# A two-block transformer on one core: seven block products in place of eight in every second pair of feed-forward up slots

## The reference, cut to what matters

```python
def swiglu(x, w_gu, w_down):
    g, u = jnp.split(x @ w_gu, 2, axis=-1)
    return (jax.nn.silu(g) * u) @ w_down
...
    for i in range(DEPTH):
        h = h + 0.5 * swiglu(rmsnorm(h, ffn1_norm[i]), ffn1_w_gu[i], ffn1_w_down[i])
        ...
        h = h + 0.5 * swiglu(rmsnorm(h, ffn2_norm[i]), ffn2_w_gu[i], ffn2_w_down[i])
        ...
    for l in range(DEPTH_2):
        mod = jax.nn.silu(c) @ ada_w[l] + ada_b[l]
```

## Time and profile before

| | |
|---|---|
| median of three runs | 3028.4 us (3027.08 to 3031.49) |
| the profiled execution, its time | 3027.1 us |
| the profiled execution, its span | 3025.4 us |
| mean granted TensorE clock | 0.995 |
| PE matmul busy | 2989.9 us, 99% |
| DVE busy | 1691.3 us, 56% |
| ACT busy | 1104.4 us, 37% |
| POOL busy | 303.9 us, 10% |

### The profile page before, as it was taken

How to read it: one execution, slowest core, us unless ns; L and a number is a source line. 1 busy time by engine, 2 the same in 40 slices (tenths; PEclk the granted TensorE clock), 3 DMA queues, 4 the chain that set the end, 5 groups by cost and what they waited for, 6 DMA issues and landing times.

```text
span 3025.4 us, 36951 instructions
## 1 busy us (share of the span) xinstructions
PE 2989.9 (99%) x13582; PEld 2432.9 (80%) x13582; DVE 1691.3 (56%) x2381; ACT 1104.4 (37%) x1717; POOL 303.9 (10%) x248
## 2 busy tenths in 40 slices
PE   8999999999999999999999999999999999999999
PEld 7888888778888887888888888888888775688887
DVE  6655564565655557555456455555556767463334
ACT  4232333562332234322232454232323555552223
POOL 2000300000100012000030000200003215600000
PEclk9999999999999999999999999999999998999999
DMA  5332232123323223432232212333222420122232
GB/s 199 109 125 95 94 98 78 58 60 115 139 97 139 97 87 95 152 139 97 92 97 96 84 38 78 111 139 141 96 97 84 170 70 29 43 79 96 95 94 82
DMA packets 86804, 301.55 MB, mean 100 GB/s; under 512 B 10272, under 2 KB 19616, under 8 KB 85536
## 3 DMA queue, kind: packets, MB, share of 16 engines
q1 hardware_dynamic: 86688, 300.02, 30.0%
HBM read 297.88 MB, written 2.10 MB: 99 GB/s over the span
## 4 chain that ended last, share of the span: by engine, by line
PE 93%; DVE 3%; ACT 2%; POOL 1%; issue 1%; DMA 0%; DVEq 0%; SPq 0%; ACTq 0%
PE proj L1194 27%; PE proj L1196 27%; PE proj L1195 27%; PE ot L1341 1%; PE proj L1575 1%; PE proj L1577 1%; PE proj L1576 1%; DVE w_lo L1688 1%; PE sc L1575 1%; PE sc L1577 1%; PE sc L1576 1%; POOL work L644 1%; PE ot L1468 0%; PE tr L1301 0%; PE sc L1290 0%
## 5 line engine op out<-in xcount | busy, mean ns | idle before, releaser
L1194 PE MATMUL proj<-u_hi,w_hi 128*128 128x512 f32 x2632 | 1029.5, 391 | 13.6 <-DVE u_lo L1693 9.0
L1196 PE MATMUL proj<-u_hi,w_lo 128*128 128x512 f32 x2632 | 1021.6, 388 | 0.0
L1195 PE MATMUL proj<-u_lo,w_hi 128*128 128x512 f32 x2632 | 1021.6, 388 | 0.0
L1688 DVE TENSOR_TENSOR w_lo<-raw,w_hi 128x1024 fp32r<-128x1024 f32 (+4 forms) x567 | 657.2, 1162 | 492.1 <-ACT w_hi L673 482.9
L673 ACT ACTIVATE w_hi<-raw 128x1024 fp32r<-128x1024 f32 (+4 forms) x567 | 535.9, 954 | 334.9 <-PE proj L1196 212.9
L1194 PEld LDWEIGHTS proj<-u_hi,w_hi 128*128 128x128 f32 x2632 | 494.8, 188 | 122.8 <-issue 15.9
L1195 PEld LDWEIGHTS proj<-u_lo,w_hi 128*128 128x128 f32 x2632 | 495.0, 188 | 104.1 <-issue 3.1
L1196 PEld LDWEIGHTS proj<-u_hi,w_lo 128*128 128x128 f32 x2632 | 494.7, 188 | 101.9
L1194 PE MATMUL proj<-a_hi,w_hi 128*128 128x512 f32 x936 | 368.1, 393 | 3.4 <-DVE w_lo L1688 1.5
L1196 PE MATMUL proj<-a_hi,w_lo 128*128 128x512 f32 x936 | 364.9, 390 | 0.0
L1195 PE MATMUL proj<-a_lo,w_hi 128*128 128x512 f32 x936 | 364.5, 389 | 0.0
(11 more groups left out here) (469 smaller groups left out, 2879.7 us busy)
## 6 DMA issues: line engine op xcount, KB each, us to landing
raw<-in_ffn_gu SPq DMA_DIRECT2D x174, 512.0 KB, 3.4
raw<-in_in_w SPq DMA_DIRECT2D x68, 512.0 KB, 3.3
raw<-in_ffn_dn SPq DMA_DIRECT2D x64, 512.0 KB, 3.3
raw<-in_ff SPq DMA_DIRECT2D x64, 512.0 KB, 3.4
gate<-in_ada SPq DMA_DIRECT2D x8, 3072.0 KB, 12.0
raw<-in_ffn_dn SPq DMA_DIRECT2D x32, 384.0 KB, 3.0
raw<-in_in SPq DMA_DIRECT2D x18, 512.0 KB, 3.4
raw<-in_mla_out SPq DMA_DIRECT2D x16, 512.0 KB, 3.4
```

The costliest lines, as they stand in the source:

```text
L1194: pe.matmul(out, w_h, x_h, start=first, stop=False)
L1195: pe.matmul(out, w_h, x_l, start=False, stop=False)
L1196: return pe.matmul(out, w_l, x_h, start=False, stop=last)
L1688: dve.tensor_tensor(wt(w_lo, slot, slot.tiles), wt(raw, slot, slot.tiles), wt(w_hi, slot, slot.tiles).bitcast(F32), ALU.subtract).then_inc ...
```

## The change

Every second tile in the up rounds of the four blocks is worked as a 2x2 block product after Strassen, in Winograd's form. The two slots of the tile (gate and up) and their common input are cut in two along the input features, the input also along the tokens: A11, A12 are the gate's upper and lower 512 features, A21, A22 those of the up slot, and the input has four quarters of 4 tiles x 256 tokens. Seven products replace eight; each has 4 k tiles, three matmuls a tile, 256 columns.

A pair needs four sums of weights, S1 to S4 (`block_sums` on DVE, four operations of 128x512), which are split like weights (`sums_hi` on ACT, `sums_lo` on DVE, two operations of 128x1024 each). Of the ordinary splits A11 with A12 (`gate_hi`, `gate_lo`, 128x1024) and A22 (`up_hi`, `up_lo`, 128x512) stay, A21 needs none. Each block needs four differences of input quarters once, split too: `diffs` has 18 operations on DVE (ten of 128x1024, eight of 128x512), `diffs_hi` five copies on ACT. Partial results are copied out of PSUM by ACT (`part_copy`, four of 128x256) and added by DVE while it reads the banks (one of 128x512, two of 128x256), then scaled by the inverse norm at once (128x1024).

Which rounds: in block one the first group stays as it was, in blocks two to four there is no such group. The group that follows begins with two ordinary rounds, in which DVE and ACT also work off `diffs` and `diffs_hi`, one quarter of them in each of the four tiles. All later rounds have one pair (gate and up by seven products) and one ordinary tile (`gate2`, `up2`). That makes 2 + 3 pairs in block one and 2 + 4 + 3 in each of the others, 32 in all.

The room for the differences comes from `work`, `sq`, `acc` and the end of `gate_t`. For that `ada_w` comes in twelve loads of four rows (2 MB), one in every group, reduced in the first four down slots, and the load of `p` for the last stage of a layer moves from before `mix_out` to after the second block's last down loads, behind a wait for that block's up slots. Some semaphores of the second model are merged into counters (`late_made`, `late_turned`, `pool_late`, `act_late`). The rounds with pairs are written out on DVE and ACT and are a loop on PE.

```diff
-ADA_BATCH = 6
+ADA_BATCH = 4
...
+def start_group(no):
+    return 1 if no == 0 else 0
+def ordinary_rounds(no, g):
+    return FF_GROUPS[g] // 2 if g < start_group(no) else 2 if g == start_group(no) else 0
+def paired_rounds(no, g):
+    return FF_GROUPS[g] // 2 - ordinary_rounds(no, g)
...
+    def sums_hi(p):
+        for i, at in enumerate((P_S1, P_S4)):
+            act.wait_ge(block_sum, 4 * p.number + 4)
+            act.activation(p.place(w_hi, at, 2), p.place(w_sum, at, 2), ACT.Copy).then_inc(block_hi, 1)
+    def gate_hi(p):
+        act.wait_ge(raw_in[p.gate.pos], p.gate.loads)
+        act.wait_ge(*p.place_free(3))
+        act.activation(p.place(w_hi, P_A11, 2), wt(raw, p.gate, KD), ACT.Copy).then_inc(w_hi_ready, 1)
...
+    def part_copy(p, i):
+        product, bank = ((0, sum_banks[3]), (4, sum_banks[3]), (6, sum_banks[3]), (3, sum_banks[1]))[i]
+        if product == 6:
+            act.wait_ge(slot_done, p.up.done)
+        else:
+            act.wait_ge(*p.done(product))
+        if i == 0:
+            act.wait_ge(slot_read, p.gate.free + 1)
+        act.activation(part_at(i), bank, ACT.Copy).then_inc(part_copied, 1)
...
+    def paired(layer, f, g, a_hi_before):
+        down = [Slot(layer, STAGE[f"ffn{f + 1}_down{g}"] + j) for j in range(AHEAD)]
+        pairs = pairs_of(layer, f, g)
+        for n, p in enumerate(pairs):
+            after = pairs[n + 1] if n + 1 < len(pairs) else None
+            up_hi(p)
+            part_copy(p, 0)
+            inner_hi(p, 0)
+            if n:
+                inner_a_hi(pairs[n - 1])
+            elif a_hi_before:
+                a_hi_before()
+            inner_hi(p, 1)
+            part_copy(p, 3)
+            part_copy(p, 1)
+            part_copy(p, 2)
+            act.wait_ge(pair_scaled, p.number + 1)
+            act.activation(pair_th, both[:, 0:S], ACT.Tanh, scale=0.5).then_inc(tanh_ready, 1)
+            if after:
+                sums_hi(after)
+            else:
+                split_hi(down[0])
+            act.wait_ge(act_ready, p.count)
+            act.activation(a_hi(p.tile), both[:, S:2 * S], ACT.Copy).then_inc(a_hi_ready, 1)
+            if after:
+                gate_hi(after)
+            else:
+                split_hi(down[1])
+            act.wait_ge(slot_read, p.gate2.done)
+            act.activation(work(4), work(3), ACT.Tanh, scale=0.5).then_inc(tanh_ready, 1)
+        inner_a_hi(pairs[-1])
...
+            def up(it, last=False):
                 for q in range(2):
                     entry = isinstance(it, int) and it + q == 0
                     opened = OPENED if first and isinstance(it, int) and it == 0 else RING if passed and entry else 0
+                    if last and q:
+                        sums_hi(Pair(layer, f, g, 0))
+                    elif 2 * q + AHEAD >= opened:
                         split_hi(Slot(layer, s0 + 2 * q + AHEAD, it, RING))
                     gated = Slot(layer, s0 + 2 * q, it, RING)
                     act.wait_ge(slot_read, gated.done)
                     act.activation(work(2 + q), work(q), ACT.Tanh, scale=0.5).then_inc(tanh_ready, 1)
+                    if last and q:
+                        gate_hi(Pair(layer, f, g, 0))
+                        return
                     if 2 * q + 1 + AHEAD >= opened:
                         split_hi(Slot(layer, s0 + 2 * q + 1 + AHEAD, it, RING))
+                    a_hi_of(it, q)
+                    if starts:
+                        diffs_hi(no, 2 * it + q)
...
+    def diffs_hi(no, i):
+        if i == 0:
+            act.wait_ge(x_diff, XD * no + 3)
+            act.activation(d_at(xd_r, 0), d_at(xd_f, 1), ACT.Copy).then_inc(x_diff_hi, 1)
+        elif i == 1:
+            act.wait_ge(x_diff, XD * no + 5)
+            act.activation(d_at(xd_r, 2), d_at(xd_f, 3), ACT.Copy).then_inc(x_diff_hi, 1)
+        elif i == 2:
+            act.wait_ge(x_diff, XD * no + 11)
+            act.activation(d_at(xd_r, 4)[:, 0:S], t3_raw(0), ACT.Copy)
+            act.activation(d_at(xd_r, 4)[:, S:2 * S], t3_raw(1), ACT.Copy).then_inc(x_diff_hi, 1)
+        else:
+            act.wait_ge(x_diff, XD * no + 13)
+            act.activation(t4_hi, t4_raw, ACT.Copy).then_inc(x_diff_hi, 1)
...
+    def pair_products(p):
...
+        pe.wait_ge(w_lo_ready, p.gate.done)
+        pe.wait_ge(slot_read, p.gate.free + 1)
+        for i, (at, bank, x, opens) in enumerate(((P_A11, b0, of_u(0, 0), True), (P_A12, b1, of_u(1, 0), True),
+                                                  (P_A22, b3, of_diff(3), True), (P_S1, b2, of_diff(0), True),
+                                                  (P_S2, b0, of_diff(1), False), (P_S4, b2, of_u(1, 1), False),
+                                                  (P_S3, b0, of_diff(2), False))):
+            if i == 2:
+                pe.wait_ge(w_lo_ready, p.up.done)
+                pe.wait_ge(x_diff, XD * (p.no + 1))
+            if i == 3:
+                pe.wait_ge(block_lo, 2 * p.number + 1)
+            if i == 5:
+                pe.wait_ge(block_lo, 2 * p.number + 2)
+            if i in (4, 5, 6):
+                pe.wait_ge(part_copied, p.copied + i - 3)
+            w_h, w_l = p.place(w_hi, at), p.place(w_lo, at)
+            for k in range(KD // 2):
+                cols = slice(k * P, (k + 1) * P)
+                pe.matmul(bank, w_h[:, cols], x[0](k), start=opens and k == 0, stop=False, skip_group_check=True)
+                pe.matmul(bank, w_h[:, cols], x[1](k), start=False, stop=False, skip_group_check=True)
+                mm = pe.matmul(bank, w_l[:, cols], x[0](k), start=False, stop=k == KD // 2 - 1, skip_group_check=True)
+            mm.then_inc(product_done if i < 5 else slot_done, 1)
...
+    def block_sums(p):
...
+        dve.wait_ge(*p.place_free(2))
+        dve.tensor_tensor(s1, a21, a22, ALU.add).then_inc(block_sum, 1)
+        dve.tensor_tensor(s3, a11, a21, ALU.subtract).then_inc(block_sum, 1)
+        dve.wait_ge(block_sum, 4 * p.number + 1)
+        dve.tensor_tensor(s2, s1, a11, ALU.subtract).then_inc(block_sum, 1)
+        dve.wait_ge(block_sum, 4 * p.number + 3)
+        dve.tensor_tensor(s4, a12, s2, ALU.subtract).then_inc(block_sum, 1)
...
+    def diffs(no, i):
...
+        def step(to, x, y, op):
+            if at[0] > XD * no:
+                dve.wait_ge(x_diff, at[0])
+            at[0] += 1
+            dve.tensor_tensor(to, x, y, op).then_inc(x_diff, 1)
+        if i == 0:
+            if no == 0:
+                dve.wait_ge(sin_ready, 1)
+            step(four(t1), u_of(u_hi_t, 0, 1), u_of(u_hi_t, 0, 0), ALU.subtract)
+            step(four(t2), u_of(u_lo_t, 0, 1), u_of(u_lo_t, 0, 0), ALU.subtract)
+            step(t1, t1, t2, ALU.add)
+            step(four(t2), u_of(u_hi_t, 1, 1), four(t1), ALU.subtract)
+            step(four(t2), four(t2), u_of(u_lo_t, 1, 1), ALU.add)
+        elif i == 1:
+            for j in range(2):
+                k = slice(2 * j, 2 * j + 2)
+                spare = t4_raw[:, 0:S]
+                step(four(t3_raw(j)), u_of(u_hi_t, 1, 1)[:, k], u_of(u_hi_t, 0, 1)[:, k], ALU.subtract)
+                step(four(spare), u_of(u_lo_t, 1, 1)[:, k], u_of(u_lo_t, 0, 1)[:, k], ALU.subtract)
+                step(t3_raw(j), t3_raw(j), spare, ALU.add)
+        elif i == 2:
+            step(four(t4_raw), u_of(u_hi_t, 1, 0), four(t2), ALU.subtract)
+            step(four(t4_raw), four(t4_raw), u_of(u_lo_t, 1, 0), ALU.add)
+            for n in range(2):
+                dve.wait_ge(x_diff_hi, XH * no + n + 1)
+                step(d_at(xd_r, 2 * n + 1), d_at(xd_f, 2 * n + 1), d_at(xd_r, 2 * n).bitcast(F32), ALU.subtract)
+        else:
+            dve.wait_ge(x_diff_hi, XH * no + 3)
+            for j in range(2):
+                step(t3_lo(j), t3_raw(j), d_at(xd_r, 4)[:, j * S:(j + 1) * S].bitcast(F32), ALU.subtract)
+            dve.wait_ge(x_diff_hi, XH * no + 4)
+            step(t4_lo, t4_raw, t4_hi.bitcast(F32), ALU.subtract)
...
+    def paired(layer, f, g, norm, before):
+        down = [Slot(layer, STAGE[f"ffn{f + 1}_down{g}"] + j) for j in range(AHEAD)]
+        pairs = pairs_of(layer, f, g)
+        for n, p in enumerate(pairs):
+            after = pairs[n + 1] if n + 1 < len(pairs) else None
+            if n:
+                normed(pairs[n - 1].up2, work(5), norm).then_inc(slot_read, 1)
+            up_lo(p)
+            if n:
+                inner_act(pairs[n - 1])
+            elif before:
+                before[0]()
+            dve.wait_ge(*p.done(1))
+            dve.wait_ge(part_copied, p.copied + 1)
+            dve.tensor_tensor(both[:, 0:HALF], sum_banks[0], part_at(0), ALU.add)
+            sums_lo(p, 1)
+            split_lo(p.gate2)
+            if n:
+                inner_a_lo(pairs[n - 1])
+            elif before:
+                before[1]()
+            split_lo(p.up2)
+            dve.wait_ge(slot_done, p.up.done)
+            dve.wait_ge(part_copied, p.copied + 4)
```

(110 more changed lines are left out.)

272 lines of the change are left out of this document (176 added, 96 removed).

## The result

The changed kernel takes 3076.9 us (median of 4 runs, 3075.7 to 3077.1) against 3027.9 us before: 1.0159 times as long, 95% interval 1.0141 to 1.0176. The forecast was 3070, range 3040 to 3090.

A forecast was written before the change was run, and what follows sets the result against it. TensorE's instruction count was taken to bound the kernel (busy 99%). Opening waits of +68.5 us less 26.6 saved by pairs gave +41.9 on 3027.1, so 3069, or 3070 for the median; range 3040 to 3090.

The forecast's parts named there:

- A pair saves 0.83: TensorE: 84 matmuls of 256 columns (10.05 us) replace 48 of 512 (10.89 us); 32 pairs save 26.6 us.
- Rival 4: TensorE's narrow matmuls have no fixed part, 0.1134 us each: 17 us less, 3053 us; chance 3%.
- Prices on VectorE: Time per VectorE operation: dependent steps 1.27 us for 1024 elements, 0.73 for 512; independent ones 1.14 and 0.61.
- set 0: First set of input differences in VectorE's queue in a block's opening rounds: five 1024 steps, 6.22 us.
- set 1: Second set of input differences in VectorE's queue, between the splits of slots 4 and 6: 4.26 us.
- set 2: Third set of input differences in VectorE's queue, between the split of slot 6 and the weight sums: 4.95 us.
- Rival 2: VectorE does the new sums at two results a cycle: 28.4 us less in all, 3041 us; chance 9%.
- Opening rounds: Two rounds opening each block: differences in VectorE's queue make TensorE wait, 68.5 us together over four blocks.
- Paired rounds hide everything: Rounds with a pair, 20.94 us on TensorE: VectorE's and ScalarE's chains end 0.56 and 0.47 us early, no wait.
- Rival 1: The paired rounds wait too: at 1 us for each of 21 rounds, 3091 us; chance 16%.
- Rival 3: Opening rounds: differences fill VectorE's idle time for ScalarE; if all of it, waits 9.5 us, time 3011; chance 8%.
- The rest at nothing: Smaller `ada_w` loads, moved row products, later load of `p`, merged counters and fewer ScalarE table loads cost no time.

The follow-up runs named there:

- experiment 6: Changed kernel with its differences in their old places but without a single pair, every slot by eight products: 3078.5 us, 1.0164 of the kernel before.
- experiment 2: Changed kernel with the same operations in the same two opening rounds, the differences spread to where VectorE waits for ScalarE: 3051.3 us, 1.0081 of before.
- experiment 4: Changed kernel without the four modulation row products in the third group's down slots, their loads kept: 3071.0 us, 1.0144 of the kernel before.

## Why the prediction was right, step by step

- **A pair saves 0.83.** Right in kind; 0.78. The 84 matmuls take the 0.1197 us of the earlier trace rows, but the change from 512 to 256 columns and back adds the rest (10.08 + 10.90 against 21.77). 32 pairs: 25.0 in place of 26.6. Rival 4 falls: 84 matmuls in 10.08 us are 0.12 each. By the formula that the prediction weighed from the Trainium skill ("TensorE: Matmul & The Clock Gate", section "Back-to-back issue gap") a pair would save an estimated 1.18 us (32 pairs 37.8, not 37.6). The page gives it for a matmul by itself, not for a stream with weight loads; here 0.1197 us stands against its 0.109.
- **Prices on VectorE.** Dependent 1024 steps follow each other after 1.25 us (1.27 taken), set 0 takes 6.17 (6.22), set 1 4.23 (4.26), set 2 5.05 (4.95). Rival 2 (two results a cycle) falls: 1.22 us for 1024.
- **Opening rounds.** Forecast 68.5, measured 68.8 with the delay of the block ends in it. By block: 13.5, 17.6, 20.0, 17.6 against 12.96, 17.92, 19.70, 17.92. The composition differs. In the second block the waits are 4.27 at slot 4 (4.58), 0.70 at slot 6 (2.76), 8.09 at the pair (8.50) and none at the third product (2.08). The missing 2.06 and 2.08 are there as slow running: 13.52 us from 817.64 to 831.16 where two slots and the wait take 11.58, and 12.55 for the first pair in place of 10.08. VectorE's and ScalarE's chain sets the later times, so what TensorE loses to its clock it doesn't wait for. That is why the total held; without such a chain behind it the clock adds to the sum (experiment 6). The prediction had this for the first pair, not for slots 4 and 6. At the third product the agreement is in part luck: VectorE has its operands ready at 855.34, and TensorE at its slow pace comes at 855.73, so there the clock and no longer VectorE sets the time.
- **Paired rounds hide everything.** Right, no wait at a later pair; VectorE is busy for 78% of the first paired round (16.44 of 21.00 us) and 64% of a later one, 75% forecast. The margin was less than thought: `gate_lo` starts at 957.86, so it is done for TensorE at 959.13 (+1.23 + 0.04), and the pair starts at 959.38, 0.25 early (0.56 taken), because VectorE's first sum starts 1.04 us behind the seventh product's end (949.51, 948.47), not 0.62. Rival 1 was near and didn't come.
- **Rival 3** (ScalarE gets ahead, the other side) falls: the waits came. That the idle places can be filled is true all the same, if the order puts the differences into them (experiment 2).
- **The rest at nothing.** Here the prediction failed in size. The rows in the third group's down slots were put into VectorE's waiting time at 1.2 us; they take up to 2.06 beside POOL's squares, and cost 1.25 us in each last stage and 0.8 at the end of the first block (experiment 4). The load of `p` did cost nothing.
- **The 7.6 us between the sum and the spans' difference** (49.5 - 41.9) are the pairs' 1.6, the last stages' 2.5, the second model's 2.9, and 0.6 in small pieces. In the second model 1.6 us of the 2.9 are a slow stretch behind a 2.08 us wait that both kernels have; why the rest moves by 1 to 2 us between kernels with the same work there is open.

## What to carry to other kernels

Seven products in place of eight do save time, if the extra sums lie where the vector engine waits for another engine anyway: 0.78 us of 10.89 a pair. By the count alone it would be an eighth, 1.36; matmuls of half the width took more than half the time (0.1197 against 0.2268 us). The same sums in line ahead of the next weight split cost 68.8 us here, against a gain of 25.0. Price work by the place: what ends last in that stage, what stands behind it in the queue, and which engine reads the same memory beside it. A wait of some microseconds on TensorE can cost more than its length when nothing else is late behind it, since the clock falls: 30.6 us of waits made 49.0 in experiment 6.
